# Neighbourhood attention on one core: three buffers instead of two for position bias and mask, the sums one unit further ahead on GpSimd

## The reference

```python
# latent: each query sees 8 x 16 neighbours and 256 cached context keys, in one softmax
bias = rpb[:, dr_i, dc_i]                       # learned relative position bias
s_loc = einsum(q, k_gathered) + bias
s_loc = where(valid, s_loc, -inf)
s_ctx = einsum(q, k_ctx)
p = softmax(concatenate([s_loc, s_ctx]))
o = p[..., :nk] @ v_gathered + p[..., nk:] @ v_ctx
# context tokens: plain attention over the 256 context tokens
```

## Time and profile before

| what | us |
|---|---|
| median of three runs | 3791.66 |
| the profiled execution | 3793.69 |
| its span in the trace | 3791.9 |
| TensorE busy, of the span | 3603.6 (95%) |
| GpSimd busy, of the span | 1230.1 (32%) |
| attention stage, from 2303 to 2676 in the span | 373 |

### The profile page before, as it was taken

One profiled execution on the slowest core, in us unless ns is written; L12 is line 12 of the kernel. 1 busy time (PEld: TensorE's weight loads), 2 busy tenths in 40 slices (PEclk: granted clock), 3 DMA queues, 4 the chain that ended last, 5 costly groups with the idle time before them and its releaser, 6 DMA issues. The chain is left out here.

```text
span 3791.9 us, 47285 instructions
## 1 busy us (share of the span) xinstructions
PE 3603.6 (95%) x19244; PEld 3074.2 (81%) x19244; DVE 1523.5 (40%) x2472; ACT 1033.7 (27%) x1552; POOL 1230.1 (32%) x813
## 2 busy tenths in 40 slices
PE   8999998989999999999989998999899999999997
PEld 6788887768788888888868877888778888888885
DVE  2775553664334444344441014777240222111116
ACT  1441111232511111111252224777343111111113
POOL 1531113633422222222361214666253222222223
PEclk9999999999999999999989998999999999999998
DMA  3253323744122222222243456776201111111111
GB/s 118 87 168 119 106 91 132 255 150 156 43 64 70 81 67 73 67 67 67 67 161 128 152 176 164 178 174 158 84 29 39 34 39 39 39 39 34 39 39 61
DMA packets 173366, 365.38 MB, mean 96 GB/s; under 512 B 16839, under 2 KB 98247, under 8 KB 171496
## 3 DMA queue, kind: packets, MB, share of 16 engines
q1 hardware_dynamic: 167720, 352.01, 29.2%
q10 hardware_dynamic: 5440, 10.49, 0.9%
HBM read 284.84 MB, written 77.59 MB: 96 GB/s over the span
## 5 line engine op out<-in xcount | busy, mean ns | idle before, releaser
L148 POOL TENSOR_TENSOR w_lo<-w_raw,w_hi 128x1024 fp32r<-128x1024 f32 x207 | 501.7, 2424 | 1487.1 <-ACT w_hi L142 1487.1
L156 PE MATMUL ps_r<-a_hi,w_hi 128*128 128x512 f32 (+1 forms) x2496 | 643.8, 360 | 17.1 <-POOL a_lo L1796 9.8
L156 PE MATMUL ps_r<-a_lo,w_hi 128*128 128x512 f32 (+1 forms) x2496 | 638.7, 358 | 0.0
L156 PE MATMUL ps_r<-a_hi,w_lo 128*128 128x512 f32 (+1 forms) x2496 | 638.2, 357 | 0.0
L156 PEld LDWEIGHTS ps_r<-a_hi,w_hi 128*128 128x128 f32 x2496 | 417.3, 189 | 100.8 <-POOL a_lo L1796 17.6
L142 ACT ACTIVATE w_hi<-w_raw 128x1024 fp32r<-128x1024 f32 x207 | 217.7, 1052 | 989.7 <-PE ps_r L156 567.0
L156 PEld LDWEIGHTS ps_r<-a_lo,w_hi 128*128 128x128 f32 x2496 | 417.3, 189 | 74.7 <-issue 1.8
L156 PEld LDWEIGHTS ps_r<-a_hi,w_lo 128*128 128x128 f32 x2496 | 416.9, 189 | 74.2
L1989 DVE TENSOR_TENSOR hid_l<-hid_l,ps_r 128x1280 f32<-128x1280 f32 x44 | 65.5, 1488 | 843.6 <-PE ps_r L156 843.6
L2009 DVE SCALAR_TENSOR_TENSOR x_t_l<-ps_r,mod,x_t_l 128x1024 f32<-128x1024 f32 (+1 forms) x288 | 241.4, 880 | 266.0 <-PE ps_r L156 266.0
L1836 POOL TENSOR_TENSOR hid_lo_l<-hid_l,hid_hi_l 128x1280 fp32r<-128x1280 f32 x42 | 134.6, 3205 | 491.3 <-ACT hid_hi_l L1737 491.3
(11 more groups left out here) (249 smaller groups left out, 6060.0 us busy)
## 6 DMA issues: line engine op xcount, KB each, us to landing
w_raw<-in_w_all SPq DMA_DIRECT2D x213, 512.0 KB, 3.6
ada_w_l<-in_ada_t SPq DMA_DIRECT2D x59, 512.0 KB, 3.5
v_hl<-v_d SPq DMA_DIRECT2D x128, 128.0 KB, 2.9
t_tail_f<-in_ada_t SPq DMA_DIRECT2D x24, 512.0 KB, 4.1
spec<-gout_f SPq DMA_DIRECT2D x80, 128.0 KB, 2.1
g_spec_c<-spec ACTq DMA_DIRECT2D x20, 512.0 KB, 4.6
v_d<-z_v_l SPq DMA_DIRECT2D x10, 1024.0 KB, 4.9
q_hl_l<-q_d SPq DMA_DIRECT2D x32, 320.0 KB, 6.7
```

The costliest lines, as they stand in the source:

```text
L148: pool.tensor_tensor(wl[:, s, 0:width], raw[:, s, 0:width], wh[:, s, 0:width].bitcast(F32), ALU.subtract).then_inc(w_split, 1)
L156: last = pe.matmul(out[:, c0:c1], w[:, c % 2, blk * 128:blk * 128 + 128], x[:, c0:c1], start=start and b == 0 and term == 0, stop=stop and ...
```

## The change

Three buffers instead of two for the sum, chosen by the running number of the unit modulo 3; the small tile `stat` moves behind them. `bias_mask` for unit u now waits for the reading of the unit three before it, and each call takes the unit one further on: in step g GpSimd now has `bias_mask(2g+5)`, `norm(2g+2)`, `bias_mask(2g+6)`, `norm(2g+3)`.

```diff
-            bm = place("bias_m", 57344, [128, 2, 640])
-            stat = place("stat", 62464, [128, 4, 4])
+            bm = place("bias_m", 57344, [128, 3, 640])
+            stat = place("stat", 65024, [128, 4, 4])
...
                 def bias_mask(i, u):
...
-                    if u >= 2:
-                        pool.wait_ge(sm_ok, unit_at(i, u - 1))
+                    if unit_at(i, u) >= 3:
+                        pool.wait_ge(sm_ok, unit_at(i, u - 2))
                     first = i * 128 + 128 * (u // U) + 128 * hh
                     if u % 10 == 0 and first:
                         pool.wait_ge(b_in[hh], first)
                     x = BIAS_X[j]
-                    pool.tensor_tensor(bm[:, u % 2, 256:640].rearrange("p (r c) -> p r c", c=32),
+                    pool.tensor_tensor(bm[:, unit_at(i, u) % 3, 256:640].rearrange("p (r c) -> p r c", c=32),
...
                 def prologue():
                     pool.memset(bm[:, :, 0:256], 0.0)
-                    for u in range(3):
+                    for u in range(4):
                         bias_mask(0, u)
                     norm(0, 0)
-                    bias_mask(0, 3)
+                    bias_mask(0, 4)
                     norm(0, 1)

                 def step(i, g, last):
                     for half in range(2):
-                        if not (last and g >= G - 2):
-                            bias_mask(i, 2 * g + 4 + half)
+                        if not (last and 2 * g + 5 + half >= U):
+                            bias_mask(i, 2 * g + 5 + half)
                         if scored(g, last):
                             norm(i, 2 * g + 2 + half)
...
-                    dve.tensor_tensor_reduce(out=pb[:, u % U % 4, 0:w], in0=ps_s[u % 2][:, 0:w], in1=bm[:, u % 2, 0:w],
+                    dve.tensor_tensor_reduce(out=pb[:, u % U % 4, 0:w], in0=ps_s[u % 2][:, 0:w], in1=bm[:, unit_at(i, u) % 3, 0:w],
```

## The result

The changed kernel takes 3804.58 us (median of 5 runs, 3801.43 to 3808.54), the kernel before in the same measurement 3789.45 (5 runs). The ratio is 1.0043, 95% interval 1.003 to 1.0057, that is 11 to 22 us; the two medians differ by 15.1 us.

What follows compares the result with a forecast made beforehand. TensorE was taken to set the attention stage's pace, 41.5 us busy per 45.1 us pair. First pair 5.0, norm 7 8.1 and norm 17 3.9 make 17.0: 3810.7, or 3808.7 as median; range 3799 to 3821.

Steps and rivals of the forecast that it cites:

- Equal waits in equal places, only the holes move: GpSimd's order: index and wait both move by one, so only places without a sum shift, to ahead of norms 5, 6, 15, 16.
- sums made earlier free GpSimd: Rival: sums leave their place ahead of norms 2, 3, 12 and 13, winning 17.7 us, 3774; chance 0.04.
- Norms 5 and 15, no gain: These norms lose the sum ahead of them, but TensorE reaches their transposes later anyway; taken as 0, bound 0.88 us.
- Norm 17, 3.9 us: Sum of unit 20 goes ahead of norm(17), starting it 0.56 us later in seven pairs: 3.9 us.
- Norm 7, pairs two to eight, 8.1 us: Norm(7) queues behind the sum of unit 10 and its wait for the head 1 table: 8.1 us, 3.2 of it order.
- First pair, 5.0 us: Very late table holds norm(7) 9.5 us; `mix` of group 3 4.0 late, plus 3.1 low clock, less 2.1 returned: 5.0.
- The rival of the clock: TensorE's clock also falls at norm 7 in later pairs, 3 to 4 us each: 3817.7; chance 0.10.
- The rival of slack in TensorE, no change: Work behind the transposes of units 7 and 17 is late anyway and swallows the delays: 3791.7; chance 0.09.
- The small edits: Memset grows from 0.52 to about 0.8 us, prologue has one more sum ahead of norm(0); taken as 0, bound 0.9.

Runs made afterwards that it cites:

- hold_both: Changed kernel, but the sums of units 10 and 20 called behind norm(7) and norm(17), not ahead; 3788.24 us, ratio 1.0002 to the kernel before.
- lead_as_slack: Kernel before with its order of calls kept, but three buffers and each sum's wait relaxed by one unit; 3785.73 us, ratio 0.9999 to the kernel before.
- hold_10: Changed kernel, but only the sum of unit 10 called behind norm(7), unit 20 still ahead of norm(17); 3792.31 us, ratio 1.0008 to the kernel before.
- table_early: Changed kernel, but SyncE loads the head 1 bias table earlier, right after the first v block; 3794.04 us, ratio 1.0012 to the kernel before.
- hold_20: Changed kernel, but only the sum of unit 20 called behind norm(17), unit 10 still ahead of norm(7); 3799.95 us, ratio 1.0029 to the kernel before.
- norms_first: Changed kernel, but in each step GpSimd makes both norms first and the two sums behind them; 3776.16 us, ratio 0.9976 to the kernel before.

## Why the prediction was right

It said 3808.7, in 3799 to 3821, slower; 3804.58 was measured. The mechanism is the one it gave, and the experiments show each part of it. The closeness of the sum is in part luck: some of its places came out too high and others too low, as said below. Point by point, by its own steps:

- **Equal waits in equal places, only the holes move.** Shown by hold_both (all of the loss gone) and lead_as_slack (a wait relaxed without effect). The rival "sums made earlier free GpSimd" falls with the same two. GpSimd's wait for VectorE did not shrink (37.8 to 40.8 us).
- **Norms 5 and 15, no gain.** hold_both, where neither has a sum ahead of it, has pairs of 45.1 us like the kernel before.
- **Norm 17, 3.9 us.** Each gap grew by 0.52, times 7 is 3.6; hold_10 gives 3.3 by the stage. The 0.56 was a little high, since the next instruction on GpSimd starts 0.77 behind a norm's start, not 0.80.
- **Norm 7, pairs two to eight, 8.1 us.** The gaps are 1.65, 1.64, 2.21, 3.67, 2.91, 2.72 and 1.64, less 1.22 each: 0.4, 0.4, 1.0, 2.5, 1.7, 1.5 and 0.4, together 7.9. The sum is right, the places less so: the fifth to seventh pairs cost 1.7 us more than worked out (5.6 for 3.9), and the eighth was in time where 1.8 had been worked out. That these cancel is luck. table_early shows that the landing makes it. Five places wait for the table, not the seven or eight foretold, and pairs of 46.03 and 46.06 lie under the 46.3 to 47.5 given, since the table was in time there.
- **First pair, 5.0 us.** 58.12 - 53.05 = 5.1, of which 0.5 is norm(17) of that pair: 4.6. From norm(6) to `mix` of group 3 it was 12.9 us before (2321.24 to 2334.14) and 19.8 after (2316.95 to 2336.79), 6.9 late, where 4.0 + 3.1 had been worked out; the pair is 4.6 longer, so about 2.3 came back. Two terms were off by a microsecond each and cancelled. Norm(7) came 11.76 us behind norm(6), 10.5 late and not 9.5, with TensorE idle for 10.78. And from norm(7) to that `mix` it took 8.1 us (2328.71 to 2336.79), not 6.1 + 3.1 = 9.2: the granted clock fell while TensorE stood, and was 1.00 again from about 2333.8, so less of the low stretch lay on work than assumed.

This stretch shows the clock there, columns as the earlier trace rows:

```profile
2319.60:2329.50 9.90, 0.00 (x0) 0.00 (x0) 0.48 (x4) 0.00 (x0) 1.66 (x3) 0.70 1.05 225
2329.60:2333.50 3.90, 3.90 (x19) 3.90 (x20) 1.32 (x3) 1.57 (x4) 2.55 (x4) 0.50 1.05 243
```

- **The rival of the clock.** The prediction left it out of the sum, and it came true in one steady pair: the fifth is 49.56 us long, 4.45 over its 45.11 before, of which 2.5 and 0.5 are the two gaps, so about 1.5 is the low clock. The 3 to 4 us priced for it was too much. The Trainium skill ("TensorE: Matmul & The Clock Gate", on what is actually happening) says an idle array falls back to half rate, and this trace agrees, with 0.53 behind 2.69 us idle.
- **The rival of slack in TensorE, no change.** Falls: the pairs are longer by their two gaps. The fourth is 1.2 longer and not 1.5, since the kernel before has 45.40 us there and not 45.1.
- **The small edits.** The memset takes 0.74 us. From the stage's first instruction to norm(6) of the first pair it was 18.13 us before and 17.60 after, but 18.12 or 18.13 in hold_both, hold_10, hold_20 and table_early, which have the same edits. So the edits cost nothing, and the half microsecond is of this one execution.

4.6 + 7.9 + 3.6 + 1.5, less 0.3 in the fourth pair and less 0.4 from the first norm to norm(6), make the 16.8 us between the first and last norm. The total moved by 15.1, with an interval of some 5 us either way.

## What to carry to other kernels

Where an engine works through a fixed list, look at which instruction stands ahead of the one that the bounding engine waits for, and count index and wait together: a call moved ahead by one with its wait moved by one stays where it was, and only the irregular places (here units without a sum, and the first reader of a new table) change. A deeper buffer is worth something when the order uses it: the same third buffer gave nothing with the old order, went with a loss of 15 us when sums stood ahead of urgent norms, and with a gain of 0.24% when they were put behind them. What made the difference between these is the order; whether the gain needs the third buffer was not tried. An instruction that can wait for a transfer should not be put ahead of one that the bounding engine needs. And before a wait in a view is read as new, look at the same place in the kernel before: where an instruction waits for several events, the view names the last.

## What the runs showed of the hardware that was not expected

TensorE's clock fell after shorter idle times than the 2.8 us seen before, and not by their length alone. In the profile after, 2.69 us idle in the fifth pair left 0.53 of the clock for 3.4 us; in hold_20, 2.05 us idle in the sixth pair left 0.55; in the profile after, 1.93 us idle in the sixth pair left it at 1.00. The stretch behind the latter:

```profile
2567.00:2570.50 3.50, 3.42 (x30) 3.42 (x31) 1.30 (x3) 1.81 (x5) 2.69 (x5) 1.00 1.00 255
```

The first pairs show that the length does not settle it. In norms_first the scores came behind 2.14 us of waiting for k at half the clock, in lead_as_slack behind 3.09 us at nearly the full one (timeline row, then the stretch, columns as the earlier trace rows):

```profile
2322.69 2.83 PE L2206 MATMUL ps_s<-k_hl,q_hl 128*128 128x256 f32 x12 [2.14 <-DMA k_hl<-k_d]
2322.70:2325.50 2.80, 2.80 (x12) 2.63 (x12) 0.00 (x0) 0.00 (x0) 0.73 (x1) 0.50 1.07 282
```

```profile
2319.78 1.62 PE L2206 MATMUL ps_s<-k_hl,q_hl 128*128 128x256 f32 x12 [3.09 <-DMA k_hl<-k_d]
2319.80:2321.40 1.60, 1.60 (x12) 1.45 (x12) 0.00 (x0) 0.00 (x0) 0.00 (x0) 0.95 1.16 316
```

In lead_as_slack it fell only behind these scores, with TensorE idle again. What decides between such cases the runs do not show. Where it fell, a wait of 2 to 3 us cost about 1.5 us more than itself: 1.5 in the fifth pair after, 1.6 in the sixth of hold_20 (48.50 - 45.07 - 1.82). The landing of the table relative to the work is not fixed either: in the profile after, the table came in time for the sum of unit 10 in the second, third and eighth pairs, and 2 us late in the fifth.
